# Output projection: four of eight tiles as two pairs of seven products, the last two tiles' token chunks in the order 0, 2, 1, a new charge in the taps' table

## What is computed

```python
h = rms_norm(x, g_norm) * (1 + scale) + shift          # shift, scale, gate = silu(c) @ w_ada + b_ada
proj = h @ w_in                                        # 7 parts of 1024 columns
y_a = conv_branch(proj...)                             # 31 causal taps, layer norm, silu, @ w_a_out
y_b = pool_branch(proj...)                             # causal means of 2 to 16, @ w_grp, @ w_b_out
m = sigmoid(proj[..., o5:o6]) * y_a + sigmoid(proj[..., o6:]) * y_b
x = x + gate * (m @ w_out)                             # the output projection
return rms_norm(x, g_final), ...                       # and the new conv and pool states
```

## Time and profile before

| | us |
|---|---|
| median of 3 runs | 933.47 (932.53 to 934.17) |
| the profiled execution | 934.1 |
| its span | 932.3 |
| TensorE busy, matmuls | 914.5 |
| VectorE busy | 735.9 |
| ScalarE busy | 385.3 |

### The profile page before, as it was taken

The page is one execution under the profiler, slowest core; times in us unless marked ns, Lnnn a source line. Parts: engine busy times, 40 slices in busy tenths (PEclk is TensorE's granted clock), DMA queues, the critical chain, the costliest instruction groups (busy, mean ns, idle before and its releaser), DMA issues.

```text
span 932.3 us, 16713 instructions
## 1 busy us (share of the span) xinstructions
PE 914.5 (98%) x6928; PEld 896.3 (96%) x6928; DVE 735.9 (79%) x862; ACT 385.3 (41%) x540; POOL 88.5 (9%) x97
## 2 busy tenths in 40 slices
PE   7999999999999999999999999999999999999996
PEld 5699999999999999999999999999989999999996
DVE  1797999997999996999995999999897642443346
ACT  5583354434453443454433354435525321113242
POOL 0022221111021011111011210000000000000000
PEclk9999999999999999999999999999999999999998
DMA  9869989889688989799897984458851623152105
GB/s 368 341 159 231 251 214 259 225 254 241 162 224 251 256 235 266 171 243 260 242 269 235 235 194 141 140 171 287 355 227 49 250 102 146 46 189 85 46 1 182
DMA packets 77885, 191.20 MB, mean 205 GB/s; under 512 B 11633, under 2 KB 18289, under 8 KB 73841
## 3 DMA queue, kind: packets, MB, share of 16 engines
q1 hardware_dynamic: 48320, 119.61, 37.2%
q0 software_dynamic: 19328, 46.17, 24.7%
q10 hardware_dynamic: 10160, 24.35, 7.4%
HBM read 164.14 MB, written 80.49 MB: 262 GB/s over the span
## 4 chain that ended last, share of the span: by engine, by line
PE 80%; DVE 13%; DMA 4%; issue 1%; ACT 0%; SPq 0%; DVEq 0%; ACTq 0%
PE ps L918 16%; PE ps L912 16%; PE ps L914 16%; PE ps L849 10%; PE ps L852 10%; PE ps L850 10%; DVE conv_y L1641 5%; DMA ada_raw<-w_ada 2%; DVE hr L1520 1%; DMA raw<-w_sums 1%; DMA bf<-y_conv 1%; DVE stage_hi L1720 1%; DVE gr L1660 1%; PE ps L779 1%; PE ps L785 1%
## 5 line engine op out<-in xcount | busy, mean ns | idle before, releaser
L1641 DVE SCALAR_TENSOR_TENSOR conv_y<-conv_u,par_all,conv_y 128x1024 f32<-128x1024 f32 x240 | 300.4, 1277 | 2.1 <-DVE conv_y L1627 0.6
L914 PE MATMUL ps<-tr,hr 128*128 128x258 f32 x824 | 216.4, 283 | 0.0
L912 PE MATMUL ps<-tr,hr 128*128 128x258 f32 x824 | 215.5, 283 | 0.3 <-ACT u L1281 0.3
L918 PE MATMUL ps<-tr,hr 128*128 128x258 f32 x824 | 166.3, 283 | 0.0
L1215 ACT ACTIVATE hr<-raw 128x512 fp32r<-128x512 f32 (+1 forms) x188 | 115.7, 618 | 116.2 <-PE ps L918 87.4
L912 PE MATMUL ps<-hr 128*128 128x258 f32 x616 | 160.9, 282 | 1.3 <-DVE pool_u L1545 1.0
L914 PE MATMUL ps<-hr 128*128 128x258 f32 x616 | 161.5, 283 | 0.0
L912 PEld LDWEIGHTS ps<-tr,hr 128*128 128x128 f32 x824 | 156.9, 190 | 0.5 <-issue 0.5
L914 PEld LDWEIGHTS ps<-tr,hr 128*128 128x128 f32 x824 | 155.7, 189 | 0.0
L1520 DVE TENSOR_TENSOR hr<-raw,hr 128x512 fp32r<-128x512 f32 (+1 forms) x188 | 125.6, 672 | 5.3 <-ACT hr L1215 1.4
L918 PEld LDWEIGHTS ps<-tr,hr 128*128 128x128 f32 x824 | 127.2, 188 | 0.0
(11 more groups left out here) (200 smaller groups left out, 1272.4 us busy)
## 6 DMA issues: line engine op xcount, KB each, us to landing
w_sums<-w_main POOLq DMA_DIRECT2D x56, 512.0 KB, 9.3
raw<-w_sums SPq DMA_DIRECT2D x104, 256.0 KB, 4.6
raw<-w_main SPq DMA_DIRECT2D x82, 256.0 KB, 4.9
w_sums<-w_sums POOLq DMA_DIRECT2D x26, 512.0 KB, 5.5
w_raw<-w_main SPq DMA_DIRECT2D x24, 512.0 KB, 4.9
w_sums<-w_main ACTq DMA_DIRECT2D x22, 512.0 KB, 5.3
ada_raw<-w_ada SPq DMA_DIRECT2D x8, 1024.0 KB, 21.0
bf<-x_t SPq DMA_DIRECT2D x4, 1032.0 KB, 8.1
```

The costliest lines, as they stand in the source:

```text
L912: nc.tensor.matmul(bank[:, c, :], wh[:, w_cols], x_hi[:, k, t_cols], start=start and k == 0, stop=False, skip_group_check=True)
L914: nc.tensor.matmul(bank[:, c, :], wh[:, w_cols], x_lo[:, k, t_cols], start=False, stop=False, skip_group_check=True)
L918: last = nc.tensor.matmul(bank[:, c, :], wl[:, w_cols], x_hi[:, k, t_cols], start=False, stop=(k == n_k - 1), skip_group_check=True)
L1641: ins = v.scalar_tensor_tensor(out=y, in0=conv_u[:, x, k:k + SEQ], scalar=par_all[:, g, x, k:k + 1], in1=y, op0=ALU.mult, op1=ALU.add)
```

## The change

In the output projection tiles 0 and 1 stay plain jobs. Tiles 2, 3 and 4, 5 become two pairs (`OUT_A`, `OUT_B`) of seven products each, `OUT_ITEMS`. They use w_hi/w_lo as a ring of four quarters, `raw5` slots 0 to 3, and new operand sums `out_tf`/`out_tr` made of m by VectorE and ScalarE at the stage's start. Their weight sums are a 14th chunk in `w_sums`. x comes in row by row (`load_x`), into `stage_lo` for tiles 0 to 5. The last two tiles are taken as 7, then 6, and their chunks as 0, 2, 1 (`LAST_ORDER`). Squares are added from one buffer, with a new semaphore `x_new_added`. In the taps' table slot 0 is charged `first_value`. The variance sums move from steps 3 and 5 to 5 and 7, and the last two additions to `row_mean` move up among the sums.

```diff
+SUM_CHUNKS = N // 2 + 1
...
+OUT_TILE = {OUT_A: 2, OUT_B: 4}
+OUT_ITEMS = [("P1", OUT_A), ("P1", OUT_B), ("P6", OUT_A), ("P2", OUT_A), ("P7", OUT_A), ("P5", OUT_A), ("P4", OUT_A), ("P3", OUT_A),
+             ("P6", OUT_B), ("P2", OUT_B), ("P7", OUT_B), ("P5", OUT_B), ("P4", OUT_B), ("P3", OUT_B)]
+OUT_AT = {item: i for i, item in enumerate(OUT_ITEMS)}
+FIRST_STRASSEN = JOB_OUT + 2
...
+OUT_T_LO = ["P6", "P7", "P5", "P4"]
...
-COST = {"lo": 580, "half": 680, "tap": 1165, "first_tap": 1900, "last_tap": 2270, "level": 1130, "out": 2100, "pool_lo": 1150, "mix": 1370}
+COST = {"first_value": 1470, "lo": 580, "half": 680, "tap": 1165, "first_tap": 1900, "last_tap": 2270, "level": 1130, "out": 2100, "pool_lo": 1150, "mix": 1370}
...
+    if slot == 0:
+        return COST["first_value"]
+    form, n = ITEMS[slot - 1]
...
-MEAN_AT = {3 * 9 + 1: 0, 3 * 9 + 2: 1, 3 * 12 + 1: 2, 3 * 12 + 2: 3}
+MEAN_AT = {3 * 9 + 1: 0, 3 * 9 + 2: 1, 3 * 12 + 1: 2, 3 * 12 + 2: 3, 3 * 13 + 1: 4, 3 * 13 + 2: 5}
...
+LAST_ORDER = [0, 2, 1]
...
+        out_tr = [at("out_tr_h", [2, 2, KH, HALF], F32R, zone_h), at("out_tr_b", [2, 2, KH, HALF], F32R, zone_b)]
+        out_tf = [at("out_tf_h", [2, 2, KH, HALF], F32, zone_h), at("out_tf_b", [2, 2, KH, HALF], F32, zone_b)]
+        u2_out, u3_out = row_mean[:, 0:HALF], row_mean[:, HALF:TOK]
+        sq_tile = pool_s1[:, 0:TOK]
...
+        def x_res(m):
+            return stage_lo[:, m % 2, :] if m < KT - 2 else hf[:, m - (KT - 2), :]
...
+        def raw_slot(q):
+            return (q - OUT_SPLIT) % 4 if q >= OUT_SPLIT else q % RAW_SLOTS
...
+            def load_out_item(i):
+                form, n = OUT_ITEMS[i]
+                if i < 4:
+                    sp.wait_ge(w_lo_done, lo_count(JOB_OUT + i // 2))
+                else:
+                    sp.wait_ge(item_lo, OUT_SPLIT + i - 3)
...
+            load_x(0)
+            load_x(1)
+            for i in range(4):
+                load_out_item(i)
+            sp.wait_ge(x_new_ready, 1)
+            load_x(2)
+            sp.wait_ge(x_new_ready, 2)
+            load_x(3)
+            for i in range(4, len(OUT_ITEMS)):
+                load_out_item(i)
+            sp.wait_ge(x_new_ready, 3)
+            load_x(5)
+            sp.wait_ge(x_new_ready, 4)
+            load_x(4)
+            sp.wait_ge(item_lo, OUT_SPLIT + 12)
...
-            for step in range(3 * (N // 2) + 3):
+            for step in range(3 * SUM_CHUNKS + 3):
...
-            for r in range(4, 6):
-                add_row(r)
...
-                if k == 3:
+                if k == 5:
...
-                if k == 5:
+                if k == 7:
...
-            job_pairs(JOB_OUT + 1, 4, m_hi, m_lo)
-            single(JOB_OUT + 5, m_hi, m_lo)
+            single(JOB_OUT + 1, m_hi, m_lo)
...
+            for i, (form, n) in enumerate(OUT_ITEMS):
+                pe.wait_ge(item_lo, OUT_SPLIT + i + 1)
+                if form == "P1":
+                    pe.wait_ge(dve_evac, FIRST_STRASSEN - 1 + (n - OUT_A) - JOB_B)
+                    block_product(OUT_SPLIT + i, bank_a(n), gr[:, 0:KH, HALVES[0]], gr[:, KT:KT + KH, HALVES[0]], start=True).then_inc(item_done, 1)
+                if form == "P2":
+                    pe.wait_ge(seeded, n + 1)
+                    block_product(OUT_SPLIT + i, bank_b, gr[:, KH:KT, HALVES[0]], gr[:, KT + KH:2 * KT, HALVES[0]]).then_inc(item_done, 1)
+                if form == "P3":
+                    pe.wait_ge(c22_out, n + 1)
+                    block_product(OUT_SPLIT + i, bank_c, gr[:, KH:KT, HALVES[1]], gr[:, KT + KH:2 * KT, HALVES[1]]).then_inc(item_done, 1)
+                if form == "P6":
+                    pe.wait_ge(seeded, n + 1)
+                    out_t_product(i, bank_a(n), form, n)
...
+            last_product(0, JOBS - 1)
             last_product(0, JOBS - 2)
-            last_product(0, JOBS - 1)
-            last_product(1, JOBS - 2, {SUMS_0_AT: sums_0})
-            last_product(1, JOBS - 1)
-            last_product(2, JOBS - 2, {SUMS_1_AT: sums_1})
-            last_product(2, JOBS - 1, {SPREAD_AT: lambda: spread(1)})
+            last_product(1, JOBS - 1, {SUMS_0_AT: sums_0})
+            last_product(1, JOBS - 2)
+            last_product(2, JOBS - 1, {SUMS_1_AT: sums_1})
+            last_product(2, JOBS - 2, {SPREAD_AT: lambda: spread(1)})
...
-            token_columns(2, [sq_sum, bf[:, KT - 1, :]])
+            token_columns(2, [sq_sum, bf[:, KT - 2, :]])
...
+                elif q < OUT_SPLIT + 4:
+                    act.wait_ge(pe_done, JOB_OUT + (q - OUT_SPLIT) // 2 + 1)
                 else:
-                    act.wait_ge(item_done, AT["MIX", max(MIX_IN)] + 1)
-                act.wait_ge(raw_loaded[q % RAW_SLOTS], 16 * (q // RAW_SLOTS + 1))
-                nc.scalar.activation(ring(q)[0][:, 0:n], raw5[:, q % RAW_SLOTS, 0:n], ACT.Copy).then_inc(item_hi, 1)
+                    act.wait_ge(item_done, LAST + q - OUT_SPLIT - 3)
+                act.wait_ge(raw_loaded[raw_slot(q)], raw_landed(q))
...
+            out_t_hi("P5", 1)
+            out_t_hi("P7", 2)
+            item_split(OUT_SPLIT)
+            item_split(OUT_SPLIT + 1)
+            out_t_hi("P6", 3)
+            out_t_hi("P4", 4)
+            tile_square(0, 0)
+            item_split(OUT_SPLIT + 2)
+            item_split(OUT_SPLIT + 3)
+            out_seed(OUT_A)
+            tile_square(1, 1)
+            for i, (form, n) in enumerate(OUT_ITEMS):
+                act.wait_ge(item_done, LAST + i + 1)
+                if form == "P6":
+                    if n == OUT_B:
+                        act.wait_ge(c12_out, n)
+                    nc.scalar.activation(halves(u2_out), bank_a(n), ACT.Copy).then_inc(u2_ready, 1)
+                if form == "P7":
+                    if n == OUT_B:
+                        act.wait_ge(c22_out, n)
+                    nc.scalar.activation(halves(u3_out), bank_a(n), ACT.Copy).then_inc(u3_ready, 1)
+                if (form, n) == ("P2", OUT_A):
+                    out_seed(OUT_B)
+                if i + 4 < len(OUT_ITEMS):
+                    item_split(OUT_SPLIT + i + 4)
+                if (form, n) == ("P3", OUT_A):
+                    tile_square(2, 3)
+                if (form, n) == ("P2", OUT_B):
+                    tile_square(3, 2)
+                if (form, n) == ("P5", OUT_B):
+                    last_hi(1, slice(0, KT * P), 12)
+                if (form, n) == ("P4", OUT_B):
+                    last_hi(0, slice(0, FORM_COLS), 13)
+                if (form, n) == ("P3", OUT_B):
+                    last_hi(0, slice(FORM_COLS, KT * P), 14)
...
+            def add_square(n):
+                dve.wait_ge(x_new_squared, n + 1)
+                link(v.tensor_tensor(sq_sum, sq_sum, sq_tile, ALU.add))
+                dve.sem_inc(x_new_added, 1)
...
+            def second_half(m):
+                gate = mod[:, 4 + m // 4, m % 4, :]
+                xp, xs = (hf[:, KT + m, cols_] for cols_ in (slice(HALF, SEQ), slice(SEQ, TOK)))
+                v.scalar_tensor_tensor(out=xp, in0=xp, scalar=gate[:, 0:1], in1=x_res(m)[:, HALF:SEQ], op0=ALU.mult, op1=ALU.add)
+                link(v.tensor_tensor(xs, xs, gate[:, 1:NMOD], ALU.mult))
+                link(v.tensor_tensor(xs, xs, x_res(m)[:, SEQ:TOK], ALU.add))
...
+            ot1, ot2, ot3, ot4 = (out_t(form, 1, full=True) for form in ("P5", "P6", "P7", "P4"))
+            m_rows = hf[:, KT:2 * KT, :]
+            link(v.tensor_tensor(ot1, m_rows[:, 0:KH, HALVES[0]], m_rows[:, 0:KH, HALVES[1]], ALU.subtract))
+            dve.sem_inc(t_summed, 1)
+            link(v.tensor_tensor(ot3, m_rows[:, KH:KT, HALVES[1]], m_rows[:, 0:KH, HALVES[1]], ALU.subtract))
+            dve.sem_inc(t_summed, 1)
+            dve.wait_ge(gate_ready, 2)
+            v.tensor_scalar(minus_gate[:], mod[:, 4:6, :, 0], -1.0, None, ALU.mult)
+            plain_x(0)
+            item_lo_part(OUT_SPLIT)
+            item_lo_part(OUT_SPLIT + 1)
+            link(v.scalar_tensor_tensor(out=ot2, in0=ot1, scalar=-1.0, in1=m_rows[:, KH:KT, HALVES[1]], op0=ALU.mult, op1=ALU.subtract))
+            dve.sem_inc(t_summed, 1)
+            link(v.scalar_tensor_tensor(out=ot4, in0=ot2, scalar=-1.0, in1=m_rows[:, KH:KT, HALVES[0]], op0=ALU.mult, op1=ALU.subtract))
+            dve.sem_inc(t_summed, 1)
+            out_t_lo("P6", 3)
+            plain_x(1)
+            item_lo_part(OUT_SPLIT + 2)
+            item_lo_part(OUT_SPLIT + 3)
+            out_t_lo("P7", 2)
+            out_t_lo("P5", 1)
+            add_square(1)
+            for i in range(len(OUT_ITEMS)):
+                out_result(i)
+                if i + 4 < len(OUT_ITEMS):
+                    item_lo_part(OUT_SPLIT + i + 4)
+                if i == 0:
+                    out_t_lo("P4", 4)
+                if OUT_ITEMS[i] == ("P6", OUT_B):
+                    add_square(2)
+                if OUT_ITEMS[i] == ("P7", OUT_B):
+                    add_square(3)
+                if OUT_ITEMS[i] == ("P5", OUT_B):
```

(9 more changed lines are left out.)

## The result

| | before | after |
|---|---|---|
| median, us | 933.72 (6 runs, 932.26 to 936.36) | 926.00 (6 runs, 925.60 to 930.16) |
| ratio, 95% interval | | 0.9923 [0.9906, 0.9941] |
| the profiled execution, its span | 934.1, 932.3 | 925.6, 923.8 |

The kernel is 7.7 us faster by the medians and 8.5 by the two profiled spans; 7.1 was forecast.

The account below looks back on a forecast made before the run. TensorE was taken to bound the kernel, by number of matmuls times their pitch. Gains of 5.04 + 1.85 + 0.2 = 7.1 us off the median 933.47 gave 926.4, range 924.8 to 928.9.

Parts of the forecast that it names:

- its own case: Whole kernel: the main forecast's interval, 925.7 to 927.1 us, given a chance of 0.60.
- part 1: Output projection: four wide jobs (45.44 us) become fourteen narrow products (40.40), other engines' cover costing nothing; gain 5.04 us.
- part 2: Pair stage: the new taps' table removes TensorE's early waits for pool_u and stage_hi L1545; gain 1.25 us.
- part 3: b stage: later variance sums remove a 1.70 us wait, but VectorE's low weights gate next; 1.85 us together with the table.
- part 4: Kernel's end: with the last chunks reordered, the last column sums start sooner; gain 0.2 us.
- its own sign: b stage: the variance-sum term is wrong if TensorE starts JOB_B+6 before 705.5 or after 707.
- rival A: b stage: VectorE's chain doesn't move, low weights of JOB_B+6 stay at 706.99; kernel takes 927.2 us; chance 0.12.
- C: Pair stage: the taps' shift doesn't take TensorE's early waits (1.25 us stay); kernel takes 927.2 us; chance 0.03.
- B: Head of the new output-projection stage: stall of 1 to 2 us at the fifth to seventh product; 927.4 to 928.4; chance 0.14.
- D: Output projection: narrow matmuls cost as much as wide ones, bound by weight load; slower, 939.0 us; chance 0.02.
- E: Output projection: item 4's load lands late, in 14.6 us (level) or 21.0 (939.9 us); chance 0.04.
- F: Better: VectorE's chain moves fully and products run a little quicker than 2.886 us; 925.3 us; chance 0.05.

Follow-up runs that it names:

- the two comparisons: Changed kernel against the kernel before, timed twice, the second on another chip: medians 926.00 against 933.72 us, then 925.77 against 934.37.
- added work: Changed kernel with two more VectorE additions of 1032 elements, results unused, ahead of the fifth narrow product's low weights: 931.27 us (one execution).
- the kernel with both edits: Kernel before with only the new taps' table and the variance sums moved to steps 5 and 7: 932.74 against 934.28 us, ratio 0.9981.
- the kernel with the pairs alone: Changed kernel with the old taps' table and variance sums back at steps 3 and 5, new chunk order kept: 928.54 us, ratio 0.9941; again 929.79.
- the early split: Changed kernel with weight read-out and split of JOB_B+4 to +6 one operand row sooner on ScalarE and VectorE: 925.53 us, ratio 0.9907; again 925.17.

## Why the prediction was right

The forecast of 926.4 stands against 926.0 and 925.8, inside its own case. As a gain it was low: 7.1 forecast, 7.7 and 8.6 by the medians of the two comparisons, and the parts that repeat add up to 8.0. That the first comparison came within 0.6 of the forecast is in part luck. Term by term:

| | forecast | measured | from |
|---|---|---|---|
| part 1, pairs | 5.04 | 5.04 | 56.81 - 51.77; 51.76 to 51.77 in all eight traces with the pairs and no added work |
| part 2, table | 1.25 | 1.7 to 1.8 | landmarks from 86 to 377 us, 1.71 to 1.82 in nine traces |
| part 3, variance sums | 0.60 (1.85 - 1.25) | 0.87, 0.89 | alone, and undone |
| part 4, order | 0.2 | 0.27 | undone |
| chance | 0 | +0.6 | 0.50 near 405 us, 0.29 in the last spread, -0.17 at the start |

The measured column adds up to 8.6, with part 2 at 1.81, for the 8.5 between the two profiled runs.

**Part 1.** The count of products times 2.886 held to a hundredth: the 336 narrow matmuls take 40.41 us from the first to the next wide one (40.4 forecast), 120.3 ns each, and the pair stage had shown 120.2 for the same form. The line in the Trainium skill, "TensorE: Matmul & The Clock Gate", section "Back-to-back issue gap", that the prediction weighed would by its estimate have cost 1.5 us; the trace does not agree with it. The walk through VectorE's work had the slack at the fifth product right to 0.3 us. The place it had as the tightest, the second product with 0.9, is so in the trace too: tile 1's result is done at 849.20 and the product starts at 850.07; no run loaded that place. The prediction had taken a link between sums at 0.57 where this stage shows 0.15, so it erred on the careful side.

**Part 2 is the term that was mis-sized.** The step that failed is the price of the two waits: "TensorE waited 0.98 us for it: that wait goes", and with the other "Gain 1.25 us" (its own rows add up to 1.28). Both waits went, but each was worth more than its idle row: 1.28 for 0.98 (1.17 to 1.28 over the nine traces with the table), 0.53 for 0.30. VectorE's stop at 513.25 came at 511.11, 2.14 sooner, where the prediction had asked for some 1.2.

**Part 3.** "1.70 us is not the gain, since the next gate is VectorE's" is shown by the kernel with this edit alone (0.87) and by the row 0.93 for `w_lo` where some 1.1 was forecast. The start of `JOB_B`+6, 704.99, was outside my own bounds of 705.5 to 707, so by its own sign part 3 failed; the 0.9 us that the pair stage gave beyond the forecast came in with it, and without them the start is 705.88. The 0.37 that VectorE's chain was to lose by the later root (its own rows give 679.09 - 678.76 = 0.33) was at most 0.09: the sums started 0.1 to 0.2 sooner than I had counted, and the root followed by 0.78, not 0.88. In the changed kernel's trace VectorE shows no wait for the root, and its wait for `y_conv`, 0.73 in place of 0.65, accounts for the 0.08 by itself; the wait for the root is seen only in the trace of this edit alone. That its chain moves freely, against rival A, shows in the `y_conv` wait, which was 0.65 before and 0.73 after, 2.06 us sooner on the clock.

**Part 4** was 0.27 for a forecast of 0.2. The rest of what the end gave in the first two traces is the last spread, 1.31 for 1.60.

**Rivals.** A and C fall, since VectorE's chain moved by 2.05 and the early waits went. B falls, since there is no stop among the fourteen, though some 1.6 us more work would have brought one. D falls by the pitch of 120 ns. E falls, since ScalarE waited 0.95 us for the fifth product's load and TensorE never did:

```profile
853.98 1.19 ACT L1335 ACTIVATE w_hi<-raw 128x512 fp32r<-128x512 f32 x2 [0.95 <-DMA raw<-w_sums]
```

F came nearest in size, with times 0.4 and 0.6 us under the forecast, but by stops that cost more than their rows and not by quicker products.

**What stays open** is why the median of the kernel with both edits fell only 1.5 us when its trace shows 2.8 at `JOB_B`+6. Its 12 runs spread over 4 us, and the start of a run alone differs by 0.6 to 2 us between traces (below). The granted clock tells a part: four of the 12 had a mean of 0.996 or more, with a median of 931.4, against 933.6 for the 14 such runs of the 29 of the kernel before, 2.2 us. Why so few of the 12 had it is not known. The 14th chunk of sums and the reads of x row by row were not tried alone; the kernel with the pairs alone has them, and its pair stage shows no loss that repeats.

## What to carry to other kernels

Before a stop is counted as a gain, find the next gate behind it and the distance to it: here 1.70 us of wait gave 0.87, and moving that next gate gave 1.17 more for a one-line edit. Work that is counted in matmuls of a form already in the trace was priced here to a hundredth, so the care belongs to the cover: walk the other engines through the new stretch; the slack came out right to some 0.3 us here. A single pair of traces mixed in chance of 0.6 us here, and the start alone of another 4.8; the same landmark in several builds separates it from the edit.

## What the runs showed of the hardware

**A stop of TensorE cost about 0.25 us more than the idle on its row** (0.19 to 0.31), for rows of 0.26 to 0.98 us: 1.17 to 1.28 for 0.98 (`pool_u`), 0.53 for 0.30, 1.16 and 1.18 for 0.93 (`w_lo`), 0.85 for 0.60 (the stop at 439.55), 0.50 for 0.26 (the stop at 441.50), 1.15 for 0.84 (the added work). The rows of the `w_lo` stop show where it lies. The second matmul starts 0.26 us after the first where the pitch is 0.16, 0.10 more. And the idle is counted from the modelled end of the matmul before the stop, 0.32 after its start, where the next would have started after 0.16: 0.16 more. The granted clock was 1.00 at all these stops.

**The granted clock varied at both ends of the kernel, also between two executions of one program.** The last spread took 1.09 us in eight of the thirteen traces, at a mean of 0.86 to 1.00 over the two microseconds from its start, and 1.31 to 1.95 in the five where that was 0.51 to 0.68. The window that begins with the spread (us, busy of PE, PEld, DVE, ACT, POOL, granted clock, DMA share, GB/s), the changed kernel with the early split:

```profile
915.74:917.74 2.00, 1.09 (x8) 0.93 (x8) 0.87 (x2) 0.00 (x0) 0.00 (x0) 1.00 0.89 315
```

and the kernel with the order undone:

```profile
916.26:918.26 2.00, 1.95 (x8) 1.72 (x8) 0.02 (x1) 0.00 (x0) 0.00 (x0) 0.51 0.86 311
```

A mean of 0.51 is nearly all at the lower of the two levels, 1.2 in place of 2.4 GHz. In both, TensorE had done one-column matmuls and then stood 0.65 us, so these rows do not tell why the two differ. At the start the kernel with the added work had a mean of 0.66 from 30 to 40 us:

```profile
30.00:40.00 10.00, 7.83 (x33) 7.74 (x32) 6.97 (x13) 4.66 (x9) 1.57 (x2) 0.66 0.81 304
```

against 1.00 in the changed kernel. It stood 4.8 us behind at 86 us and ended 5.7 us behind, 1.15 of which is the added work: this is why its 931.27 says nothing of the slack. Smaller dips, to a mean of 0.91 between 20 and 40 us, went with 0.6 to 1.0 us in four other traces and 2.0 in a fifth; the two of the kernel with the early split were among them. In the other seven traces the mean there was 1.00, and they reached the same place within 0.22 us of each other. That the lower clock is the cause of the lost time, and not a sign of waits that came first, is argued and not shown: in the two slowest starts TensorE also waited 2.1 and 2.2 us near 32 us for VectorE's `hr`, where it is 0.63 at most in the others.

**Loads in the pair stage landed unevenly.** The seven traces with the same instructions up to 405 us gained between 0.17 and 0.54 us there against the kernel before, and three of the thirteen fell back between 439 and 464 us, by 0.85, 0.50 and 0.23. The median from issue to landing of the weight sums' loads was 4.9 us in one trace of the changed kernel and 4.8 in the other.
